# Running sums of stick-breaking attention: one fp32 product against two rounded ones

## What is computed

```python
def stick_breaking_attention(q, k, v):          # per head; T = 528 = 16 + 512
    z = einsum('bhqd,bhkd->bhqk', q_blk, kh) * D ** -0.5
    visible = key_pos[None, :] < q_pos[:, None]
    log_keep = where(visible, log_sigmoid(-z), 0.0)
    log_w = log_sigmoid(z) + cumsum(log_keep, axis=3, reverse=True) - log_keep
    w = where(visible, exp(log_w), 0.0)
    return einsum('bhqk,bhkd->bhqd', w, vh)
```

## Time and profile before

| | |
|---|---|
| median of 3 runs | 2877.83 us (2876.08 to 2878.53) |
| the profiled execution | 2880.18 us |
| its span | 2878.4 us |
| TensorE busy | 2767.6 us, 96% |
| VectorE busy | 1346.9 us, 47% |
| ScalarE busy | 737.0 us, 26% |
| GpSimd busy | 1625.1 us, 56% |
| mean granted TensorE clock | 0.982 of full speed |
| the eight heads of the stick-breaking part | about 712 to 800 us of the span |

### The profile page before, as it was taken

The page is one execution under the profiler, slowest core; times in us unless marked ns, Lnnn a source line. Parts: engine busy times, 40 slices in busy tenths (PEclk is TensorE's granted clock), DMA queues, the critical chain, the costliest instruction groups (busy, mean ns, idle before and its releaser), DMA issues.

```text
span 2878.4 us, 39917 instructions
## 1 busy us (share of the span) xinstructions
PE 2767.6 (96%) x15611; PEld 2248.5 (78%) x15611; DVE 1346.9 (47%) x1964; ACT 737.0 (26%) x1142; POOL 1625.1 (56%) x1569
## 2 busy tenths in 40 slices
PE   8999989999999999999999999999999898999999
PEld 7988888899688878888865478888777455788887
DVE  6797563422710564333346633331276678433311
ACT  3386224642620111110036621110111222211100
POOL 7653115765077766666641157676675535676764
PEclk9998999999999999999999999999999999999999
DMA  4221001222023565655530013332322100233331
GB/s 131 76 72 36 2 2 45 88 89 74 1 88 102 194 202 165 194 182 190 183 103 16 30 59 103 95 101 101 104 88 92 37 1 15 88 102 88 108 101 69
DMA packets 292585, 260.22 MB, mean 90 GB/s; under 512 B 6617, under 2 KB 264390, under 8 KB 292156
## 3 DMA queue, kind: packets, MB, share of 16 engines
q1 hardware_dynamic: 289492, 250.83, 27.1%
q0 software_dynamic: 2416, 6.34, 0.7%
q10 hardware_dynamic: 504, 0.66, 0.1%
HBM read 255.72 MB, written 2.10 MB: 90 GB/s over the span
## 4 chain that ended last, share of the span: by engine, by line
PE 84%; DVE 8%; issue 4%; DVEq 2%; ACT 2%; POOL 0%; DMA 0%; ACTq 0%; POOLq 0%; SPq 0%
PE ps L539 23%; PE ps L540 23%; PE ps L541 23%; PE ps L1786 2%; DVE cv L2366 1%; PE ps L1627 1%; PE ps L1764 1%; PE ps L1607 1%; PE ps L1617 1%; PE ps L1749 1%; PE ps L1371 1%; PE ps L1350 1%; PE ps L951 1%; DVE YB L2933 1%; PE ps L1378 1%
## 5 line engine op out<-in xcount | busy, mean ns | idle before, releaser
L829 POOL CAST spl<-raw 128x512 fp32r<-128x512 f32 (+1 forms) x352 | 252.2, 717 | 625.2 <-PE ps L541 489.3
L539 PE MATMUL ps<-HSH,spl 128*128 128x512 f32 x1344 | 535.5, 398 | 21.2 <-DVE HSL L750 16.3
L831 POOL TENSOR_TENSOR spl<-raw,spl 128x512 fp32r<-128x512 f32 (+1 forms) x352 | 501.9, 1426 | 56.2 <-issue 6.4
L540 PE MATMUL ps<-HSL,spl 128*128 128x512 f32 x1344 | 526.7, 392 | 0.0
L541 PE MATMUL ps<-HSH,spl 128*128 128x512 f32 x1344 | 526.4, 392 | 0.0
L835 POOL TENSOR_TENSOR spl<-raw,spl 128x512 fp32r<-128x512 f32 (+1 forms) x352 | 488.7, 1388 | 51.5 <-issue 1.3
L539 PE MATMUL ps<-HNH,spl 128*128 128x264 f32 (+1 forms) x1152 | 359.8, 312 | 3.4 <-DVE HNL L720 2.9
L540 PE MATMUL ps<-HNL,spl 128*128 128x264 f32 (+1 forms) x1152 | 357.2, 310 | 0.0
L541 PE MATMUL ps<-HNH,spl 128*128 128x264 f32 (+1 forms) x1152 | 356.5, 309 | 0.0
L833 POOL CAST spl<-raw 128x512 fp32r<-128x512 f32 (+1 forms) x352 | 234.1, 665 | 196.4 <-PE ps L541 194.2
L539 PEld LDWEIGHTS ps<-HSH,spl 128*128 128x128 f32 x1344 | 254.0, 189 | 96.7 <-issue 38.4
(11 more groups left out here) (471 smaller groups left out, 4456.1 us busy)
## 6 DMA issues: line engine op xcount, KB each, us to landing
adw<-in_ada_w SPq DMA_DIRECT2D x96, 512.0 KB, 5.4
raw<-in_w_in SPq DMA_DIRECT2D x44, 1024.0 KB, 5.1
raw<-in_ffn_w_up SPq DMA_DIRECT2D x88, 512.0 KB, 4.6
raw<-in_w_ffn_in SPq DMA_DIRECT2D x44, 512.0 KB, 4.6
raw<-in_ffn_w_down SPq DMA_DIRECT2D x16, 1408.0 KB, 5.9
raw<-in_hy_w_in SPq DMA_DIRECT2D x12, 1024.0 KB, 4.9
raw<-in_w_ffn_out SPq DMA_DIRECT2D x8, 1408.0 KB, 6.8
raw<-in_w_branch_dn SPq DMA_DIRECT2D x8, 1024.0 KB, 4.9
```

The source lines that it names most:

```text
L539: pe.matmul(dst, w[0], x[0], start=first, stop=False)
L540: pe.matmul(dst, w[0], x[1], start=False, stop=False)
L829: pool.tensor_copy(hi[:, first, :], w[:, first, :])
L831: pool.tensor_tensor(lo[:, first, :], w[:, first, :], hi[:, first, :], ALU.subtract).then_inc(split_first, 1)
```

## The change

`sbn` is split into a rounded high part `sbh` and a low part (`sbl0` for block 0, `sbl1` for the rest). ScalarE makes the high part by two rounding copies in a new step `sb_hi(n)`, VectorE the low part by two subtractions in `sb_lo(n)`. `sb_soft(n)` is cut into two instructions, 512 and 832 columns, and the five small adds and `sbr` go. `sb_sums(n)` uses a rounded `tril_r` (copied once) and rounded ones: for each block, in the order of the keys, two products with its own high and low part, and two with ones for every later block. That is 30 rounded products of 5568 columns in place of twelve fp32 ones of 2176. `sb_hi(n+1)` stands on ScalarE between weights(n) and out(n-1), `sb_hi(0)` behind log(0); `sb_lo` stands on VectorE behind `sb_soft`. The buffers move: `sbn` and `tril_r` to the place of the norm's squares, `sbl1` to the unused tail of the raw weight slots.

```diff
-        sbn = fresh("sbn", SBW)
-        SB_FROM = {4: 0, 3: 16, 1: 160}
-        sbr = fresh("sbr", 432)
+        sbh = fresh("sbh", SBW, dtype=F32R)
+        sbl0 = fresh("sbl0", SEQ, dtype=F32R)
+        sbl1 = at("sbl1", [2, SLOT], raw_at, dtype=F32R)[:, :, KD * 256:KD * 256 + 416]
+        sbn = at("sbn", [SBW], norm_at)
+        tril_r = at("tril_r", [P], norm_at + SBW, dtype=F32R)
+        SB_CHAIN = [0, 1, 3, 4, 2]
...
             def sb_sums(n):
-                pe.wait_ge(sb_n, n + 1)
+                pe.wait_ge(sb_r, 2 * n + 1)
                 if n:
                     pe.wait_ge(sb_lw, 2 * n)
-                for t, a in ((0, 1), (1, 3), (2, None), (3, 4), (4, 2)):
-                    dst = sb_bank(3, t)
-                    mm = pe.matmul(dst, tril, sb_cols(sbn, t), start=True, stop=a is None)
-                    if a is not None:
-                        x, q = sb_cols(sbn, a), SB_Q[a] - SB_Q[t]
-                        alone = P if a in SB_FROM else META
-                        mm = pe.matmul(dst[:, q:q + alone], ones[:, :], x[:, 0:alone], start=False, stop=a not in SB_FROM)
-                        if a in SB_FROM:
-                            pe.wait_ge(sb_r, 3 * n + (4, 3, 1).index(a) + 1)
-                            mm = pe.matmul(dst[:, q + P:], ones[:, :], sb_later(a), start=False, stop=True)
+                for i, t in enumerate(SB_CHAIN):
+                    dst, later = sb_bank(3, t), SB_CHAIN[i + 1:]
+                    pe.matmul(dst, tril_r[:, :], sb_cols(sbh, t), start=True, stop=False)
+                    mm = pe.matmul(dst, tril_r[:, :], sb_low(t), start=False, stop=not later)
+                    if t == 0:
+                        pe.wait_ge(sb_r, 2 * n + 2)
+                    for a in later:
+                        d = dst[:, SB_Q[a] - SB_Q[t]:]
+                        pe.matmul(d, ones_r, sb_cols(sbh, a), start=False, stop=False)
+                        mm = pe.matmul(d, ones_r, sb_low(a), start=False, stop=a == later[-1])
                     if t == 0:
                         mm.then_inc(sb_c, 1)
                 mm.then_inc(sb_c, 1)
...
+            def sb_hi(n):
+                if n:
+                    act.wait_ge(sb_c, 2 * n)
+                for h, x in enumerate((slice(0, SEQ), slice(SEQ, SBW))):
+                    act.wait_ge(sb_n, 2 * n + h + 1)
+                    act.activation(sbh[:, x], sbn[:, x], ACT.Copy).then_inc(sb_ln_hi, 1)
...
             sb_log(0)
+            sb_hi(0)
             for n in range(HEADS):
                 if n + 1 < HEADS:
                     sb_evac(n + 1)
                     sb_log(n + 1)
                 sb_weights(n)
+                if n + 1 < HEADS:
+                    sb_hi(n + 1)
                 if n:
                     sb_out(n - 1)
...
             def sb_soft(n):
-                dve.wait_ge(sb_ln, n + 1)
+                dve.wait_ge(sb_ln_hi, 3 * n + 1)
+                for x in (slice(0, SEQ), slice(SEQ, SBW)):
+                    dve.scalar_tensor_tensor(sbn[:, x], sbz[n % 3][:, x], 0.0, sbe[:, x], ALU.max, ALU.add).then_inc(sb_n, 1)
+
+            def sb_lo(n):
                 if n:
                     dve.wait_ge(sb_c, 2 * n)
-                dve.scalar_tensor_tensor(sbn[:, :], sbz[n % 3][:, :], 0.0, sbe[:, :], ALU.max, ALU.add).then_inc(sb_n, 1)
-                n1, n2, n3, n4 = (sb_cols(sbn, t) for t in range(1, NT + 1))
-                s1, s3, s4 = (sb_later(t) for t in (1, 3, 4))
-                dve.drain()
-                dve.tensor_tensor(s4, n4[:, P:], n2, ALU.add).then_inc(sb_r, 1)
-                dve.tensor_tensor(s3[:, 0:P], n3[:, P:2 * P], n4[:, 0:P], ALU.add)
-                dve.tensor_tensor(s1[:, 0:P], n1[:, P:2 * P], n3[:, 0:P], ALU.add)
-                dve.drain()
-                dve.tensor_tensor(s3[:, P:], n3[:, 2 * P:], s4, ALU.add).then_inc(sb_r, 1)
-                dve.drain()
-                dve.tensor_tensor(s1[:, P:], n1[:, 2 * P:], s3, ALU.add).then_inc(sb_r, 1)
+                dve.wait_ge(sb_ln_hi, 3 * n + 2)
+                dve.tensor_tensor(sbl0[:, :], sbn[:, 0:SEQ], sbh[:, 0:SEQ], ALU.subtract).then_inc(sb_r, 1)
+                dve.wait_ge(sb_ln_hi, 3 * n + 3)
+                rest = [y[:, SEQ:SBW].rearrange("p (a n) -> p a n", a=2) for y in (sbn, sbh)]
+                dve.tensor_tensor(sbl1, *rest, ALU.subtract).then_inc(sb_r, 1)
...
+            dve.tensor_copy(tril_r[:, :], tril)
             sb_soft(0)
+            sb_lo(0)
             for n in range(HEADS):
                 if n + 1 < HEADS:
                     sb_abs_of(n + 1)
                 sb_log_w(n)
                 if n + 1 < HEADS:
                     sb_soft(n + 1)
+                    sb_lo(n + 1)
```

More of the change, by code:

```diff
@@ L417, in build @@
         sv_t, sv_done = sem("sv_t"), sem("sv_done")
-        sb_z, sb_zs, sb_abs, sb_ln = sem("sb_z"), sem("sb_zs"), sem("sb_abs"), sem("sb_ln")
+        sb_z, sb_zs, sb_abs, sb_ln_hi = sem("sb_z"), sem("sb_zs"), sem("sb_abs"), sem("sb_ln_hi")
         sb_n, sb_r, sb_c, sb_lw, sb_w, sb_o, sb_oc = sem("sb_n"), sem("sb_r"), sem("sb_c"), sem("sb_lw"), sem("sb_w"), sem("sb_o"), sem("sb_oc")
@@ L855, in sb_cols, with sb_low @@
             return x[:, SB_AT[t]:SB_AT[t] + SEQ - SB_Q[t]]
-        def sb_later(t):
-            return sbr[:, SB_FROM[t]:SB_FROM[t] + SEQ - SB_Q[t] - P]
+        def sb_low(t):
+            if t == 0:
+                return sbl0[:, :]
+            c = SB_AT[t] - SEQ
+            return sbl1[:, c // 416, c % 416:c % 416 + SEQ - SB_Q[t]]
         META_FROM = 8
@@ L2074, in sb_log @@
                 act.drain()
-                act.activation(sbe[:, :], sbe[:, :], ACT.Ln, bias=ones[:, 0:1], scale=1.0).then_inc(sb_ln, 1)
+                act.activation(sbe[:, :], sbe[:, :], ACT.Ln, bias=ones[:, 0:1], scale=1.0).then_inc(sb_ln_hi, 1)
+            def sb_hi(n):
[4 more added lines that the diff above has]
+                    act.activation(sbh[:, x], sbn[:, x], ACT.Copy).then_inc(sb_ln_hi, 1)
             def sb_weights(n):
```

## The result

The changed kernel took 2894.93 us (median of 4 runs, 2893.34 to 2896.64), the one before 2877.03 on the same occasion: 1.0058 of it, 95% interval 1.0046 to 1.0071, 17.9 us slower. Timed again on another occasion, it came out at 2891.62 against 2879.19: 1.0048 (1.0034 to 1.0062), 12.4 us. Forecast were 7.1 us and at most 2889.0: the direction was right, the size was not.

A forecast was written before the change was run, and what follows sets the result against it. TensorE was taken to set the round (9.19 us), ScalarE 0.39 behind; after the change ScalarE would. Start 1.2, rounds 5.0 and end 0.9 gave +7.1 us: 2877.83 + 7.1 = 2884.9, range 2882.3 to 2889.0.

The forecast's parts named there:

- ScalarE's own round: ScalarE's time from one head's evacuation to the next without waiting for TensorE: 8.80 us, becoming 10.13 with the two copies.
- the start of sums: In a middle head, TensorE may start the next head's running sums 9.72 us after that head's evacuation starts on ScalarE.
- 0.11 for a small rounded product: On TensorE, each of the 18 rounded products of 144 or 16 columns was taken to cost 0.11 us.
- short loads: Rival, chance 0.12: rounded weight loads hide even behind 16 columns on TensorE, so +5.8 us, 2883.6.
- fp32's price per column: Rival, chance 0.14: small rounded products on TensorE cost as much per column as fp32, +9.1 us, or +13.8.
- the start: At the first heads, head 0's copies delay head 1's evacuation on ScalarE from 723.65 to 724.83: 1.2 us.
- the chances named for "slower": Chance of over 0.2% slower (above 2883.6 us), summed over the forecast and several rivals: given as 0.74.
- In the rounds themselves I expect full clock: TensorE's clock stays at full speed between evacuations, since it is busy 88%, against 89% in a full-clock stretch before.
- I let the clock fall as before and add 1.7: At the last head's sums, TensorE idles some 3 us and its clock falls as before, costing 1.7 us.
- the first round: From head 1's evacuation on ScalarE to the next: 8.51 us before, 9.64 forecast with the copies.
- the last sums: TensorE's running sums for the last head: end at 799.41 at full clock, 5.4 us later, 7.1 with the clock's fall.
- the clock falls once more: Rival, chance 0.10: another clock fall between evacuations, or a longer one at the end, +8.1 to 8.8 us, 2886.3.

The follow-up runs named there:

- The version with both gaps filled: The changed kernel plus unread 512-column fp32 products on TensorE, one before the first sums and three before the last: 2885.57 us, 1.0028 of the kernel before.
- the version with products alone: The changed kernel with its rounded products reading one rounded softplus as both parts, no copies, subtractions or small adds: 2874.73 us, 0.9990 of the kernel before.

## Why the prediction was wrong

Right, by its own steps: ScalarE's own round, 10.13 forecast and 10.08 measured, with no wait for TensorE in the middle rounds; the copies at 0.615 and 0.885 (0.623 and 0.89 forecast), the subtractions at 0.69 and 1.03; the start of sums 9.77 after the evacuation (9.72), and the 28 rounded products behind the second wait in 3.52 us (758.68 to 762.20; 3.45 forecast), so that 0.11 for a small rounded product holds and the rivals of short loads and of fp32's price per column are out; the start, evac(1) 1.2 us later (725.67 less 723.65 and the 0.8 from before the heads) against 1.2. The version with both gaps filled adds all of that up: 5.3 us against 5.4. Two slips changed nothing in the time: the chances named for "slower" add up to 0.85, not 0.74, and ScalarE's 6.2 of 10 us (6.16 from 745 to 755) is in no row.

The step that failed is "In the rounds themselves I expect full clock", with "I let the clock fall as before and add 1.7". I compared TensorE's busy share, 89% and 88%, and took the work under it for equal. The middle rounds did run at full clock, but the changed kernel fell to half speed for 10.2 us in the first full round and again at the end. The terms: the first round 12.09 instead of 9.64, 2.4 us; the last sums 7.10 instead of 4.57 + 1.7 = 6.27, 0.8 us; the two output products behind them 7.54 instead of 5.16, 2.4 us. With the forecast 7.1 that is the 12.7 us of the trace. The rival "the clock falls once more" had the kind of loss, at 1.0 to 1.7 us instead of 5.6, and 0.10 of the chance.

What the runs show is that the gaps take part in it (filling one took away its own stretch and no other, both fillings both) and that the rounded products do (fp32 ones in the same gaps left at most 3.4 us), the latter from a single profile. Not settled is which gap with which products is enough. The length of the gap does not decide it: 1.11 us at the start brought 10.2 us at half speed in two profiles of the changed kernel, while 2.23 at the end of the version with products alone and 2.42 at head 1 of the one with both gaps filled, rounded products behind them too, brought nothing, and in the version with the first copy twice 1.73 us brought 10.2 us once and nothing another time. What else stood around these gaps, or when they fell, differed, and no run isolated it; nor why it is 3.4 us in the one case and 10.2 in the other. The other 5 us of the 17.9 belong to the executions and not, as far as the traces go, to the change. 3.0 are in the two profiles outside the heads: 0.8 ahead of them, 0.4 between them and the last matmul, 1.9 behind it. The second profile of the same changed kernel has the heads at the same length, 99.4 us from the first product of logits to the first GEMM product behind them against 99.3 (86.6 before the change), but they begin at 709.3 instead of 713.6, and behind the last matmul come 6.1 us instead of 8.0. The remaining 2.1 are the profiled executions' distance from their medians, 3.2 us above before the change (2880.18 against 2877.03) and 1.0 after it. The second comparison, 12.4 us, is what the heads alone account for.

## What to carry to other kernels

An operation that an engine "has time for" lengthens the round if its idle time lies inside a dependent chain: take the engine's own round, from one start to the next without the waits at its end, and compare that with the bound, not the busy share. When work is moved or split, list the gaps that TensorE will have and what it does right behind them; a gap of 1.1 us ahead of small products went with a lower clock and cost 2.5 us here, and one product that nobody reads, put into it, gave them back. Such a fall is no certainty: read the granted clock of more than one profile before pricing it. A term of a few microseconds in a kernel of thousands is found by the wait of one engine for the stage (here GpSimd's) in a profile, not by the median.

## What was unexpected of the hardware

TensorE's granted clock fell behind gaps of 1.11 and 2.83 us when rounded products of 16 to 512 columns followed, for 10.2 us, and behind gaps of 1.12 and 2.84 with fp32 products it did not fall (behind 2.89, in one version behind 2.16, and before the change behind 1.86, for 3.4 us). But behind 2.23 and 2.42 us with rounded products, in two other versions, it did not fall either, and within one trace the same gap of 1.73 us did both. A busy share near 90% told nothing of it: 0.71 and 1.00 of full speed stood at 87% and 90%. GpSimd's cast of 512 columns took 1.28 us beside VectorE's work and 0.61 without it, and VectorE's subtraction 1.26 beside GpSimd's and 0.69 without.
